# Squares of the residual for the recurrent layer's norm, taken on VectorE inside the first layer's embedding gate

## The reference, cut to what matters

```
gate = sigmoid(rms_norm(h, ple_norm[0]) @ ple_gate[0])
h = h + gate * (p[0] @ ple_proj[0])                 # end of layer 0
hn = rms_norm(h, mix_norm_pre[1])                   # start of layer 1
# rms_norm(x, g) = x * rsqrt(mean(x * x, over 1024 features) + 1e-6) * g
```

## Time and profile before

| | |
|---|---|
| Runs | 4078.36, 4087.38, 4090.19 us; median 4087.38 |
| Profiled execution, its own time | 4082.8 us |
| Span of its instructions | 4081.0 us |
| Mean granted clock of TensorE | 0.942 of full speed |
| Instructions in the trace | 65997 |

### The profile page before, as it was taken

How to read it: one execution, slowest core, us unless ns; L and a number is a source line. 1 busy time by engine, 2 the same in 40 slices (tenths; PEclk the granted TensorE clock), 3 DMA queues, 4 the chain that set the end, 5 groups by cost and what they waited for, 6 DMA issues and landing times.

```text
span 4081.0 us, 65997 instructions
## 1 busy us (share of the span) xinstructions
PE 3684.9 (90%) x28466; PEld 3299.1 (81%) x28466; DVE 1534.3 (38%) x2023; ACT 853.4 (21%) x1132; POOL 206.8 (5%) x347
## 2 busy tenths in 40 slices
PE   6999999799999998968997768888698999999977
PEld 4997348699999997844996657777497999999967
DVE  3134544522212224431337734454625221222352
ACT  2001322300000001133324423333422000001020
POOL 0000000000000000000002111111100000000000
PEclk8999999899999999986998878898899999999989
DMA  2222011111121131112325732121412112112111
GB/s 88 67 68 79 21 42 71 65 47 41 57 75 47 42 128 39 39 61 109 113 86 217 269 107 54 43 54 29 145 37 75 41 40 76 63 41 99 66 37 70
DMA packets 75366, 300.53 MB, mean 74 GB/s; under 512 B 9400, under 2 KB 11720, under 8 KB 71160
## 3 DMA queue, kind: packets, MB, share of 16 engines
q0 software_dynamic: 36816, 174.51, 11.7%
q1 hardware_dynamic: 38336, 122.87, 9.6%
HBM read 216.24 MB, written 81.10 MB: 73 GB/s over the span
## 4 chain that ended last, share of the span: by engine, by line
PE 72%; DVE 8%; issue 2%; ACT 2%; DMA 1%; POOL 0%; DVEq 0%; ACTq 0%; POOLq 0%
PE ps L447 54%; PE ps L421 3%; DVE A L1470 2%; PE ps L856 2%; PE ps L847 2%; PE ps L757 1%; DVE B L1470 1%; PE ps L461 1%; PE ps L807 1%; DVE H L1551 1%; DVE A_r L1527 1%; PE ps L870 1%; PE ps L873 1%; PE ps L479 1%; PE ps L822 1%
## 5 line engine op out<-in xcount | busy, mean ns | idle before, releaser
L447 PE MATMUL ps<-H_r,W_r 128*128 128x364 f32 (+1 forms) x3192 | 705.2, 329 | 0.0
L447 PE MATMUL ps<-H_r,TM_r 128*128 128x364 f32 x2736 | 606.7, 330 | 21.7 <-DVE A_r L1527 18.2
L447 PE MATMUL ps<-A_r,TM_r 128*128 128x364 f32 x2736 | 606.2, 330 | 0.0
L447 PEld LDWEIGHTS ps<-H_r,W_r 128*128 128x128 f32 (+1 forms) x3192 | 555.9, 188 | 1.8
L447 PEld LDWEIGHTS ps<-H_r,TM_r 128*128 128x128 f32 x2736 | 475.1, 189 | 28.2 <-issue 19.8
L447 PEld LDWEIGHTS ps<-A_r,TM_r 128*128 128x128 f32 x2736 | 476.8, 189 | 0.0
L447 PE MATMUL ps<-B_r,DW_r 128*128 128x364 f32 x2112 | 408.9, 329 | 0.0
L447 PE MATMUL ps<-B_r,W_r 128*128 128x364 f32 x1824 | 405.0, 330 | 0.0
L447 PEld LDWEIGHTS ps<-B_r,DW_r 128*128 128x128 f32 x2112 | 358.8, 188 | 0.0
L447 PEld LDWEIGHTS ps<-B_r,W_r 128*128 128x128 f32 x1824 | 319.7, 190 | 0.0
L1733 DVE TENSOR_TENSOR TM<-ps,TM 128x1092 f32<-128x1092 f32 x44 | 57.0, 1296 | 444.4 <-PE ps L447 444.4
(11 more groups left out here) (288 smaller groups left out, 4390.2 us busy)
## 6 DMA issues: line engine op xcount, KB each, us to landing
W<-in_wgu SPq DMA_DIRECT2D x88, 512.0 KB, 3.6
H<-d_h POOLq DMA_DIRECT2D x3, 4368.0 KB, 23.0
W<-in_wdown SPq DMA_DIRECT2D x32, 384.0 KB, 3.1
W<-in_wrkv SPq DMA_DIRECT2D x24, 512.0 KB, 3.6
W<-in_wdown SPq DMA_DIRECT2D x32, 320.0 KB, 2.9
d_h<-H POOLq DMA_DIRECT2D x16, 546.0 KB, 3.0
d_y<-TM POOLq DMA_DIRECT2D x16, 546.0 KB, 3.4
A<-d_y POOLq DMA_DIRECT2D x16, 546.0 KB, 7.9
```

Of the source, the lines that this page charges most:

```text
L447: ins = nc.tensor.matmul(ps[0:cols, NCH * s + c, 0:CH], w[:, j * cols:(j + 1) * cols], x[k1][:, c * CH:(c + 1) * CH], start=(k1 == 0 and n ...
```

## The change

VectorE, which in layer 0's gate has just added a tile to `H`, also squares it into `HSQ` and adds that to the running sum `HSUM` (both are tiles of `B` that are free there). For the last tile it only squares. TensorE multiplies `HSUM` and then `HSQ` by the matrix of ones, two groups of three pieces in place of eight. ScalarE's eight squares go. Semaphore names that nothing used are dropped from the list (left out below).

```diff
+        HSUM, HSQ = B[:, NP_ + KT, :], B[:, NP_ + KT + 1, :]
...
-            norm_direct()
+            s, mm, rd = t.unit()
+            pe.wait_ge(S[f"read{s}"], t.val(f"read{s}", -1))
+            for n, x in enumerate((HSUM, HSQ)):
+                pe.wait_ge(S["h_sums"], n + 1)
+                for c in range(NCH):
+                    ins = nc.tensor.matmul(ps[:, NCH * s + c, 0:CH], k("ones"), x[:, c * CH:(c + 1) * CH],
+                                           start=(n == 0), stop=(n == 1))
+            ins.then_inc(S["mm_done"], 1)
             t.up("normed", KT)
...
             log_and_exp()
-            act.wait_ge(S["h_ready"], t.val("h_ready"))
-            for j in range(KT):
-                square(H[:, j, :])
             root()
...
             def pre_norm(gain):
-                t.up("sq_ready", KT)
-                t.up("sq_used", KT)
                 rstd()
...
                         nc.vector.tensor_tensor(h, h, TM[:, j, :], ALU.add).then_inc(S["h_ready"], 1)
                         t.up("h_ready")
-
+                        if l:
+                            continue
+                        dve.wait_ge(S["h_ready"], t.val("h_ready"))
+                        if last and j == 1:
+                            nc.vector.tensor_tensor(HSQ, h, h, ALU.mult).then_inc(S["h_sums"], 1)
+                        else:
+                            step(nc.vector.tensor_tensor(HSQ, h, h, ALU.mult))
+                            step(nc.vector.tensor_tensor(HSUM, HSUM, HSQ, ALU.add))
+                        if last and j == 0:
+                            dve.sem_inc(S["h_sums"], 1)
+
+                if l == 0:
+                    step(nc.vector.memset(HSUM, 0.0))
                 with t.loop(KT // 2 - 1, mm_done=4, read0=2, read1=2, h_ready=2, chunk=4, w0=16, w1=16, w2=16, w3=16,
-                            wl_ready=2, wh=2, dve_step=2) as i:
+                            wl_ready=2, wh=2, dve_step=2 if l else 6) as i:
                     ple_tiles(i, False)
                 ple_tiles(None, True)
```

More of the change, by code:

```diff
@@ L308, in build_trunk @@
         d_v = scratch("d_v", [NPAIR, P, (NCHUNK + 1) * C])
[L311 to L316, removed]
+        names = ["setup", "held", "x_in", "mm_done", "read0", "read1", "w_used", "wl_ready", "xh_ready", "xl_ready", "h_out", "h_in", "sq_ready", "sq_used", "rs_ready", "h_sums",
+                 "normed", "h_ready", "act_step", "dve_step", "pool_step", "out_done",
+                 "wv_in", "wv_ready", "tm_free", "ax_ready", "p_in",
+                 "cum_ready", "cum_out", "cum_in", "lf_e", "logf_out", "ckt_done", "ckt_ready", "mb_done", "mb_read", "x_add", "x_ready", "v_done", "r_log", "r_ready", "qn_ready", "cumk_in", "kv_in2", "kv_in3", "turn_done", "s_done", "s_read", "e_ready",
+                 "o_read", "bias_in0", "kv_in0", "kv_in1",                  "xn_ready", "xn_tmp", "hs_out", "hs_in", "xs0", "xs1", "xs2", "xs3", "key_sq", "rk_ready", "dev_sq",
@@ L317, in build_trunk @@
                  "b_out", "key_scaled", "sum_out", "pair_done", "pair_stored", "sum_stored", "rn_used", "key_max", "key_log", "key_rn", "l_in0", "l_in1", "gn_in0", "gn_in1", "mean_in", "gn_used", "shift_in", "conv_out",
-                 "zi0", "zi1", "z_dup", "g_done", "g_ready", "m_init", "tok_done", "tok_read", "n_done", "n_ready", "mt_done", "mt_ready", "a_done", "a_ready", "u_done", "u_ready", "st_done", "oo_done", "oo_read", "st_read", "m_ready", "m0_ready", "y_done", "y_ready",
-                 "z_done", "t_done", "m_first", "c_done", "c_ready", "c_u", "c_st", "c_in", "chunk_done", "st_ready", "state_in", "state_out", "pa_done", "pb_done",
@@ L320, in build_trunk @@
-                 "y_out0", "y_out1", "y_in", "y_used", "mid_ready", "mid_hi", "mid_split", "o_all", "l_in", "l_out", "dve_p", "act_p", "pool_p", "gn_ready"]
+                 "zi0", "zi1", "z_dup", "g_done", "g_ready", "m_init", "tok_done", "tok_read", "n_done", "n_ready", "mt_ready", "a_done", "a_ready", "u_done", "u_ready", "st_done", "oo_done", "oo_read", "st_read", "m_ready", "y_done", "y_ready",
+                 "z_done", "m_first", "c_in", "st_ready", "state_in", "state_out",                  "y_out0", "y_out1", "y_in", "mid_ready", "mid_hi", "mid_split", "dve_p", "act_p", "gn_ready"]
```

## The result

The changed kernel takes 4042.47 us (median of four runs, 4037.15 to 4048.61), the kernel before beside it on the same chip 4087.47 us (4078.36 to 4090.19). The ratio is 0.9891, 95% interval 0.9872 to 0.9911.

A forecast was written before the change was run, and what follows sets the result against it. TensorE bounds the norm's serial hand-over; 17.93 us from last add to logarithm become about 4.2, 13.7 us less. That gives 4069.1 from the profiled execution, 4073.7 from the median; the middle, 4071.4 us, was forecast, range 4063 to 4081.

The forecast's parts named there:

- Removed and added on the path: 13.7 us (12.5 to 14.4).: Layer 0's norm, last add to logarithm: logarithm at 1772.32 instead of 1786.03, 13.7 us less (12.5 to 14.4).
- The square: VectorE's square of the gate's last tile, on the path: from 1768.13 to 1769.43, 1.30 us.
- the pause: TensorE idle between HSUM's records and the last square's products, 1767.2 to 1769.47: 2.3 us.
- HSQ's six records: TensorE's three fp32 products on the last tile's square, on the path: 2.83 us, ends 2.12 and 4.02.
- rival 1: Norm: all six records on the last square at 1.2 GHz, gain 12.5 us, time 4072.6; chance 0.12.
- HSUM's records done ahead: TensorE does HSUM's six records right behind the gate's last unit, 1765.37 to 1767.2, before the last square is ready.
- VectorE's work covered: Gate's first seven tiles: 2.9 us added VectorE work each, hidden by 11.0 us of cover; tiles stay 15.65 us.
- scaling beside the store: Behind the norm: scaling the eight tiles reads H while the 4.4 MB store of H runs, costed at nothing.
- rival 3: Behind the norm: scaling beside the store gives time back, gain 6.0 us, time 4079; chance 0.05.
- What is moved. All that follows starts 13.7 us earlier.: Everything behind layer 0's norm only shifts 13.7 us earlier; the pause before the next matrix product keeps its 24.9 us.
- The sign: Whole kernel's measured direction: faster 0.65, no change 0.32, slower 0.03.

The follow-up runs named there:

- the runs at equal places: Three pairs, old norm against new, with equal TensorE instruction counts modulo 256 ahead of the recurrence: new norm faster by 14.7, 10.1 and 11.4 us.
- four more squares: Changed kernel with VectorE squaring each of the gate's first seven tiles five times instead of once: 4035.23 us, ratio 0.9885 to the kernel before.
- nine more: Changed kernel with VectorE squaring each of the gate's first seven tiles ten times instead of once: 4067.57 us, ratio 0.9969 to the kernel before.
- both groups late: Changed kernel with the HSUM products also waiting for the last square, so all 12 records stand behind it: ratio 0.9891 to the kernel before.
- place 0: Kernels with as many TensorE instructions ahead of the recurrence, modulo 256, as the changed kernel, which took 4042.47 us.
- + 256: Changed kernel with 256 idle TensorE instructions added behind the norm: 4033.03 us, ratio 0.9888 to the kernel before.
- the names: Kernel before with only the changed kernel's list of semaphore names: 4080.54 us, ratio 0.9999 to the kernel before.
- after + 128: Changed kernel with 128 idle TensorE instructions added behind the norm: 4049.07 us, ratio 0.9926 to the kernel before.
- 64 places: Changed kernel with 64 idle TensorE instructions added behind the norm: 4067.85 us, ratio 0.9970 to the kernel before.
- 32 places: Changed kernel with 32 idle TensorE instructions added behind the norm: 4058.50 us, ratio 0.9954 to the kernel before.

## Why the prediction was wrong, step by step

- *Removed and added on the path: 13.7 us (12.5 to 14.4).* Right in mechanism and nearly in size: 12.9 us in the trace, 14.7, 10.1 and 11.4 us in the runs at equal places. The square took 1.30 us and the pause 2.28 us as forecast. The term that was mis-sized is HSQ's six records, 3.62 us on the chain instead of 2.83; that is nearer to rival 1's 4.02 us, and the clock was low for most of them (0.61 in the mean over the first 2 us). It isn't a fixed price: with four more squares the same six took 3.26 us after the same pause, and with nine more 2.10 us after 1.98 us. The prediction read off rows 6 that a longer pause costs more; 3.62 us after 2.28 and 2.83 after 2.51 show that the length of the pause alone does not give the price.
- *HSUM's records done ahead; VectorE's work covered; scaling beside the store.* Right, by both groups late (2.1 us more), by the four and nine more squares, and by the scaling's 10.23 us. The store, issued at 1772.80, took 12.0 us to land, and the scaling began inside it at 1779.88: rival 3 is out.
- *"What is moved. All that follows starts 13.7 us earlier."* This step failed. It took what follows as a body that only shifts in time. It also shifts in TensorE's instruction stream, by 73 places, and the recurrence's length depends on that, a term that the sum put at nothing without a reason. It measured 33.1 us in the profiled executions, whose spans differ by 34.2, and in the runs some 30 of the 45 us (45 less the 14.7 at equal places), shown by putting the 73 back (488.3 us) and by giving the old kernel 183 (453.4 us). The prediction counted instructions for what they cost where they stood and never asked what their number does to the code behind. In the kernel before, the sign was there to be read: 18.4 us on L856, 9.8 on L847 and 6.0 on L807 that TensorE waited for "issue".

The sign is the norm's: the change was faster at every place tried. The size is luck: with 64 or 32 idle instructions behind the norm the same change gains 12 or 21 us instead of 45, and nothing in the prediction chose the place.

Two things stay open. The kernels at place 0 (the changed one, + 256, both groups late, four more squares) have ratios of 0.9885 to 0.9891, each with an interval of 7 to 9 us either way, and a single profiled recurrence moved by 8.6 us with the names, so no split of the 45 us is good to better than that. And after + 128 is slower by some 10 us than its recurrence says; other loops of the kernel shift with the place too, and they were not looked at one by one.

## What to carry to other kernels

Before trusting a small gain upstream of a long TensorE loop, count how many TensorE instructions the edit adds or removes, and look for idle time by "issue" in that loop: where it returns chunk by chunk on the same operation, the layout may cost time, and a number of idle instructions ahead of the loop can be worth more than the edit (here 119 gave the old kernel 42 us and 183 gave it 36, where the edit itself is worth 10 to 15). Which number is good was found here by trying. Compare two variants whose numbers of instructions ahead of the loop are equal, or differ by a multiple of 256, or at several numbers, else the layout's 30 to 40 us is taken for the edit's.

## What the chip showed that was not expected

In the two traces TensorE stood still 0.3 to 2.8 us at a place that returns every 256 instructions, each time with a transfer of a block of instructions that had begun 2.2 to 3.1 us before its next product, and 3.3 to 4.1 us at a jump back of the loop (3.60 us at 2527.97 before). A wait of 1.52 us was followed by 1.2 GHz more often where a pause of 0.2 to 1.5 us came right behind it (six of eight, as at 2460.80 and 2488.85 before), but the same two pauses at 2701.81 were not. And nearly the same idle total can go with very different clocks: 74.4 us with 0.90 in the kernel before, 77.5 us with 0.93 at 64 places; the most idle time, 88.7 us at 32 places, came with 0.96.
